# Moving VectorE's mask of a level in a seven-level block inverse behind the add of the level before, and reordering the work between levels

## What is computed

```
first_block:  h = rms_norm(x, g_mix);  proj = h @ w_in
              y_dsa  = sparse attention, 8 heads of 128, top 64 of 256 keys
              y_rwkv = RWKV-7 recurrence, 16 heads of 64, over 256 steps
              x += concat(y_dsa, y_rwkv) @ w_out;   x += mixture of 16 experts
second_block: layer 0: gated delta rule (8 key heads, 16 value heads of 128) beside
              windowed attention (8 heads);   layer 1: short convolution
              each with its input and output projection, then a final norm
```

## Time and profile before

| what | value |
|---|---|
| median of the runs | 3404.0 us |
| the profiled execution's own time | 3401.54 us |
| its span, first to last instruction | 3399.8 us |
| PE (TensorE matmul) busy | 3102.0 us, 91% |
| PEld (weight load) busy | 2872.3 us, 84% |
| DVE (VectorE) busy | 2021.8 us, 59% |
| ACT (ScalarE) busy | 1547.8 us, 46% |
| mean granted TensorE clock | 0.971 of 2.4 GHz |

### The profile page before, as it was taken

The page is one execution under the profiler, slowest core; times in us unless marked ns, Lnnn a source line. Parts: engine busy times, 40 slices in busy tenths (PEclk is TensorE's granted clock), DMA queues, the critical chain, the costliest instruction groups (busy, mean ns, idle before and its releaser), DMA issues.

```text
span 3399.8 us, 59603 instructions
## 1 busy us (share of the span) xinstructions
PE 3102.0 (91%) x22592; PEld 2872.3 (84%) x22592; DVE 2021.8 (59%) x2817; ACT 1547.8 (46%) x2121; POOL 77.9 (2%) x98
## 2 busy tenths in 40 slices
PE   7988888869899999999798898989979899999998
PEld 6877777759799977777688888888869899999998
DVE  5766555544555688888555655656544555555544
ACT  4443333323444477767444443444424444444443
POOL 0000000001000000000000000000001000000001
PEclk9999999979999999999899999999989999999999
DMA  5422222204556699999333333334325455555554
GB/s 190 140 95 83 82 85 86 88 29 137 155 158 183 201 345 326 349 323 361 117 118 112 126 114 114 120 111 130 109 71 181 153 181 181 182 178 178 182 182 138
DMA packets 231154, 543.78 MB, mean 160 GB/s; under 512 B 16768, under 2 KB 98944, under 8 KB 231040
## 3 DMA queue, kind: packets, MB, share of 16 engines
q1 hardware_dynamic: 229664, 537.99, 47.8%
q0 software_dynamic: 656, 2.49, 0.2%
q10 hardware_dynamic: 720, 1.74, 0.1%
HBM read 540.05 MB, written 2.10 MB: 159 GB/s over the span
## 4 chain that ended last, share of the span: by engine, by line
PE 53%; issue 29%; DVE 11%; ACT 6%; DVEq 1%; POOL 0%; DMA 0%; ACTq 0%; POOLq 0%; SPq 0%
PE gp L431 14%; PE gp L432 14%; PE gp L433 14%; ACT w_hi L1050 3%; PE pm L484 2%; DVE arena L1690 2%; PE pm L478 2%; DVE w_lo L1516 1%; DVE arena L2018 1%; PE pm L470 1%; DVE arena L1535 1%; DVE arena L1681 1%; PE pm L970 0%; DVE h_both L1528 0%; PE pm L980 0%
## 5 line engine op out<-in xcount | busy, mean ns | idle before, releaser
L1516 DVE TENSOR_TENSOR w_lo<-stage,w_hi 128x1024 fp32r<-128x1024 f32 x1018 | 1238.7, 1224 | 923.7 <-ACT w_hi L1050 908.7
L1050 ACT ACTIVATE w_hi<-stage 128x1024 fp32r<-128x1024 f32 x1018 | 1071.5, 1057 | 860.0 <-PE gp L433 646.9
L431 PE MATMUL gp<-h_both,w_hi 128*128 128x256 f32 x4432 | 1301.4, 294 | 48.7 <-DVE w_lo L1516 19.7
L432 PE MATMUL gp<-h_both,w_hi 128*128 128x256 f32 x4432 | 1264.1, 285 | 0.0
L433 PE MATMUL gp<-h_both,w_lo 128*128 128x256 f32 x4432 | 1263.3, 285 | 0.0
L431 PEld LDWEIGHTS gp<-h_both,w_hi 128*128 128x128 f32 x4432 | 861.1, 194 | 72.7 <-issue 32.8
L432 PEld LDWEIGHTS gp<-h_both,w_hi 128*128 128x128 f32 x4432 | 861.5, 194 | 2.4 <-issue 1.7
L433 PEld LDWEIGHTS gp<-h_both,w_lo 128*128 128x128 f32 x4432 | 859.9, 194 | 0.0
L431 PE MATMUL gp<-y_both,w_hi 128*128 128x256 f32 x1024 | 292.2, 285 | 0.4 <-DVE y_both L1528 0.4
L432 PE MATMUL gp<-y_both,w_hi 128*128 128x256 f32 x1024 | 291.5, 285 | 0.0
L433 PE MATMUL gp<-y_both,w_lo 128*128 128x256 f32 x1024 | 291.4, 285 | 0.0
(11 more groups left out here) (468 smaller groups left out, 3451.8 us busy)
## 6 DMA issues: line engine op xcount, KB each, us to landing
stage<-in_stream SPq DMA_DIRECT2D x1018, 512.0 KB, 4.0
x<-in_x SPq DMA_DIRECT2D x4, 512.0 KB, 8.7
out<-arena SPq DMA_DIRECT2D x4, 512.0 KB, 2.6
arena<-in_lora POOLq DMA_DIRECT2D x8, 192.0 KB, 2.7
c<-in_c POOLq DMA_DIRECT2D x1, 896.0 KB, 4.8
c<-in_c ACTq DMA_DIRECT2D x1, 704.0 KB, 10.3
c<-in_c ACTq DMA_DIRECT2D x1, 640.0 KB, 7.8
vecs<-in_vecs ACTq DMA_DIRECT2D x1, 184.0 KB, 5.4
```

The source lines that it names most:

```text
L431: T.matmul(o, w_hi[:, slot, w], hi[:, k, :], start=first[t], stop=False)
L432: T.matmul(o, w_hi[:, slot, w], lo[:, k, :], start=False, stop=False)
L1050: A.activation(w_hi[:, slot, :], stage[:, k, :], ACT.Copy).then_inc(s_hi, 1)
L1516: V.tensor_tensor(w_lo[:, slot, :], stage[:, sub % SLOTS, :], w_hi[:, slot, :].bitcast(F32), ALU.subtract).then_inc(s_lo, 1)
```

## The change

VectorE's mask of level lv + 1 is issued right behind its add of level lv (`masked`), before anything else. RWKV's mask of level 0 moves ahead of the masks of R and the normed q and k; the delta rule's stays where it was, behind the same wait. What VectorE does between levels (`slot`) now stands behind that mask: in RWKV the splits stand in levels 2, 4 and 6 in place of 1, 3 and 5, ahead of `dsa(lv)`; in the delta rule they stay in 1, 3 and 5, but behind the add. The product of the cosine with q and k (line 1655) moves from `dsa(1)` to `dsa(0)`. TensorE turns the probabilities in level 6 between the turning of Y and the product (`dsa_turned`), no longer at the end of level 5. In the delta rule the two tiles at place 1 move to place 3 (`EIGHTH2`). ScalarE's program is unchanged. No instruction that computes is added or removed.

```diff
@@ -470,7 +470,7 @@
                     ins = T.transpose(o, i_, ident)
                 ins.then_inc(s, 1)
 
-            def inverse(first, state, N, C, C0, it, fill, after=None):
+            def inverse(first, state, N, C, C0, it, fill, mid=None, after=None):
 
                 for lv in range(7):
                     pe.wait_ge(s_inv, 9 * it + lv + 1)
@@ -478,6 +478,8 @@
                         ins = T.transpose(pm[:, 0, s_ * P:(s_ + 1) * P], (state if lv else first)[:, s_, :], ident)
                     ins.then_inc(s_trn, 1)
                     fill(2 * lv)
+                    if lv == 6 and mid is not None:
+                        mid()
                     pe.wait_ge(s_trno, 7 * it + lv + 1)
                     pe.wait_ge(s_blk, 7 * it + lv + 1)
                     for s_ in range(4):
@@ -488,7 +490,8 @@
                     if after is not None:
                         after(lv)
 
-            EIGHTH = {0: 0, 1: 1, 2: 2, 4: 3, 5: 4, 6: 5, 7: 6, 8: 7, 9: 8, 10: 9, 11: 10, 12: 11}
+            EIGHTH1 = {at: q for q, at in enumerate([0, 1, 2, 4, 5, 6, 7, 8, 9, 10, 11, 12])}
+            EIGHTH2 = {at: q for q, at in enumerate([0, 2, 3, 4, 5, 6, 7, 8, 9, 10, 11, 12])}
 
             pe.wait_ge(s_zero, 1)
 
@@ -542,8 +545,8 @@
                     feed(n, i, U_T1, 6, EV_T1, tiles)
 
             def feed1_eighth(at, i, last):
-                if at in EIGHTH:
-                    q = EIGHTH[at]
+                if at in EIGHTH1:
+                    q = EIGHTH1[at]
                     feed1(5 + q // 4, i, last, (q % 4 * 2, q % 4 * 2 + 2))
 
             def dsa(lv, i):
@@ -562,15 +565,16 @@
                         ins = T.matmul(pm[:, 4, qt * S:(qt + 1) * S], d_qk[:, 0, qt * P:(qt + 1) * P], d_qk[:, 1, :],
                                        start=True, stop=True)
                     ins.then_inc(sem("s_ds_sc"), 1)
-                if lv == 5:
-                    pe.wait_ge(sem("s_at_pr"), i + 1)
-                    transposes([(pm[:, 3, kt * S + qt * P:kt * S + (qt + 1) * P], d_pr[:, qt, kt * P:(kt + 1) * P])
-                                for kt in range(NT) for qt in range(NT)], sem("s_at_pT"))
                 if lv == 6:
                     pe.wait_ge(sem("s_at_pTo"), i + 1)
                     for kt in range(NT):
                         ins = T.matmul(pm[:, 4, 0:S], d_v[:, kt, :], d_pT[:, kt, :], start=kt == 0, stop=kt == NT - 1)
                     ins.then_inc(sem("s_at_o"), 1)
+
+            def dsa_turned(i):
+                pe.wait_ge(sem("s_at_pr"), i + 1)
+                transposes([(pm[:, 3, kt * S + qt * P:kt * S + (qt + 1) * P], d_pr[:, qt, kt * P:(kt + 1) * P])
+                            for kt in range(NT) for qt in range(NT)], sem("s_at_pT"))
 
             def rwkv(p, last=False):
                 pe.wait_ge(sem("s_rw_lw"), 16 * p + 16)
@@ -619,7 +623,7 @@
                     if at == 2:
                         pe.wait_ge(sem("s_rw_R"), 2 * p + 2)
 
-                inverse(r_Y, r_Y, r_N, r_C, r_C, p, fill, lambda lv: dsa(lv, p))
+                inverse(r_Y, r_Y, r_N, r_C, r_C, p, fill, lambda: dsa_turned(p), lambda lv: dsa(lv, p))
                 pe.wait_ge(s_inv, 9 * p + 9)
                 for c in range(NT):
 
@@ -893,8 +897,8 @@
                     feed(n, i, U_T2, 12, EV_T2, tiles)
 
             def feed2_eighth(at, i, last):
-                if at in EIGHTH:
-                    q = EIGHTH[at]
+                if at in EIGHTH2:
+                    q = EIGHTH2[at]
                     feed2(9 + q // 4, i, last, (q % 4 * 2, q % 4 * 2 + 2))
 
             def delta(i, last=False):
@@ -1650,9 +1654,11 @@
 
             def dsa(lv, i):
 
+                if lv == 0:
+                    dve.wait_ge(sem("s_ds_qn"), i + 1)
+                    V.tensor_tensor(d_t1, d_qn, bc(con("cos_q"), 2), ALU.mult)
                 if lv == 1:
                     dve.wait_ge(sem("s_at_rot"), i + 1)
-                    V.tensor_tensor(d_t1, d_qn, bc(con("cos_q"), 2), ALU.mult)
                     link(V.tensor_tensor(d_t2, pm[:, 3, :].rearrange("p (a b) -> p a b", a=2), bc(con("sin_q"), 2), ALU.mult))
                     V.tensor_tensor(d_qk, d_t1, d_t2, ALU.add).then_inc(sem("s_at_qk"), 1)
                     dve.wait_ge(sem("s_at_vT"), i + 1)
@@ -1673,13 +1679,12 @@
                     lower(y_lo[:, i, :], y_hi[:, i, :], pm[:, 4, 0:S], s_y)
 
 
-            def solver(Y, N, it, between, after=None, turned_first=False):
+            def masked(Y, N, it, lv):
+                dve.wait_ge(s_inv, 9 * it + lv + 1)
+                V.tensor_tensor(N, Y, bc(levels[:, lv, :], 4), ALU.mult).then_inc(s_blk, 1)
+
+            def solver(Y, N, it, slot):
                 for lv in range(7):
-                    dve.wait_ge(s_inv, 9 * it + lv + 1)
-                    if lv == 0 and turned_first:
-                        dve.wait_ge(s_trno, 7 * it + 1)
-                    V.tensor_tensor(N, Y, bc(levels[:, lv, :], 4), ALU.mult).then_inc(s_blk, 1)
-                    between(lv)
                     if lv == 6:
                         dve.wait_ge(s_inv, 9 * it + lv + 1)
                         dve.wait_ge(s_trn, 7 * it + lv + 1)
@@ -1688,8 +1693,9 @@
                     dve.wait_ge(s_inv, 9 * it + lv + (2 if lv == 6 else 1))
                     dve.wait_ge(s_prod, 7 * it + lv + 1)
                     V.tensor_tensor(Y, Y, pm[:, 1, :].rearrange("p (a b) -> p a b", a=4), ALU.add).then_inc(s_inv, 1)
-                    if after is not None:
-                        after(lv)
+                    if lv < 6:
+                        masked(Y, N, it, lv + 1)
+                    slot(lv)
 
             def rwkv(p, last=False):
                 for j in range(3):
@@ -1746,6 +1752,7 @@
                     ins = V.tensor_tensor(r_Aak[:, 2 * hd:2 * hd + 2, :], pm[:, hd, S:2 * S].rearrange("p (a b) -> p a b", a=2),
                                           bc(con("strict"), 2), ALU.mult)
                 ins.then_inc(sem("s_rw_R"), 1)
+                masked(r_Y, r_N, p, 0)
                 for hd in range(2):
                     dve.wait_ge(sem("s_rw_mR"), 2 * p + hd + 1)
                     ins = V.tensor_tensor(r_R[:, hd, :, :], pm[:, (2, 4)[hd], :].rearrange("p (a b) -> p a b", a=4),
@@ -1755,7 +1762,13 @@
                 V.scalar_tensor_tensor(d_qn[:, 0, :], d_raw[:, 0, :], vec("q_gain"), d_rs[:, 0:S], ALU.mult, ALU.mult)
                 V.scalar_tensor_tensor(d_qn[:, 1, :], d_raw[:, 1, :], vec("k_gain"), d_rs[:, S:2 * S], ALU.mult,
                                        ALU.mult).then_inc(sem("s_ds_qn"), 1)
-                solver(r_Y, r_N, p, lambda lv: feed1(5 + lv // 2, p, last) if lv % 2 else None, lambda lv: dsa(lv, p))
+
+                def slot(lv):
+                    if lv in (2, 4, 6):
+                        feed1(4 + lv // 2, p, last)
+                    dsa(lv, p)
+
+                solver(r_Y, r_N, p, slot)
                 feed1(8, p, last)
                 dve.wait_ge(sem("s_rw_mS"), p + 1)
                 for hd in range(2):
@@ -2058,7 +2071,9 @@
                 ins.then_inc(sem("s_dn_kd"), 1)
                 feed2(8, i, last)
 
-                solver(n_Y, n_N, i + RWKV_P, lambda lv: feed2(9 + lv // 2, i, last) if lv % 2 else None, turned_first=True)
+                dve.wait_ge(s_trno, 7 * (i + RWKV_P) + 1)
+                masked(n_Y, n_N, i + RWKV_P, 0)
+                solver(n_Y, n_N, i + RWKV_P, lambda lv: feed2(9 + lv // 2, i, last) if lv % 2 else None)
                 feed2(12, i, last)
 
                 dve.wait_ge(sem("s_dn_mks"), i + 1)
```

## The result

The changed kernel takes 3325.06 us (median of four runs, 3324.39 to 3326.84) against 3405.16 for the one before (four runs; the 3404.0 ahead was the median of three); the ratio of the runs is 0.9766, 95% interval 0.9749 to 0.9783. The forecast was 3331 and the profiled execution, at 3324.39 with a span of 3322.7, is 77.1 us shorter in its span than the one before.

A forecast was written before the change was run, and what follows sets the result against it. Over half the chain of waits is TensorE, idle mainly in the inverses, where VectorE's order can matter. Gains 44 + 3 + 20.9 + 4.8 = 73 us from 3401.5 give 3328.5, plus 2.5 for the median: 3331, range 3318 to 3356.

The forecast's parts named there:

- The undisturbed level: One inverse level with nothing in the way: 3.26 us in RWKV, 3.28 in the delta rule; anything above can be gained.
- The terms in an RWKV turn: Gains per level of RWKV's inverse, less a loss behind it: 6.3 us a turn, 44 over seven turns with feeds.
- Level 6: RWKV inverse, level 6: 3.92 us against 4.51, gain 0.6, with a new wait of about 0.6 before the probabilities.
- Behind the inverse: RWKV, after the last add: a split of 1.23 us before the attention output's low half, about 0.3 showing as loss.
- Turns 2, 4 and 6: RWKV turns with clock drops behind the level 1 to 2 stretch: three drops taken as gone, 4.8 us.
- Turn 7: RWKV turn without splits, clock at 0.67: only the masks count, 3 us taken, between 0 and 6.3.
- The delta rule: Its inverse's three odd levels lose a split's delay of 0.87 us each, over eight turns: 20.9; level 6 costs 0.
- Cosine product, moved fills: Cosine product in level 0's idle time; two delta tiles from place 1 to 3 fit before Y: nothing.
- A: Rival: inverse gains come, but clock drops stay (3336) or come in each turn with feeds (3355); chance 0.2.
- B: Rival: waits move to VectorE in RWKV levels 2, 4 and 6, half its gain given back, 3353; chance 0.08.
- C: Rival: levels held by ScalarE's copy and TensorE's fills alone, moved masks only change names, 3404; chance 0.03.
- D: Rival: slower, denser inverses fall to 1.2 GHz and stay there, at most 3643; chance 0.03.

The follow-up runs named there:

- Experiment two: Kernel before, with ScalarE alone rounding the halves in levels 0, 2 and 4 of both inverses, not 1, 3 and 5: 3362.53 us, ratio 0.9882.
- experiment one: Kernel before, with only the delta rule's VectorE splits of levels 1, 3 and 5 put behind add and next mask: 3383.46 us, ratio 0.9950.
- experiment ten: Changed kernel with last split behind the low half, scores moved into level 3, and probabilities divided ahead of level 6's mask in RWKV: 3315.84 us.
- six: Changed kernel with the cosine product moved back from level 0 to level 1: 3324.38 us, ratio 0.9766.
- seven: Changed kernel with the delta rule's two fill tiles back at place 1: 3324.88 us, ratio 0.9763.
- experiment three: Changed kernel with RWKV's splits in the slots of levels 1, 3 and 5 in place of 2, 4 and 6: 3336.33 us, ratio 0.9801.

## Why the prediction was right, point by point

**The undisturbed level** of 3.26, put together from 2.09 and 1.17, came out at 3.29, and the delta rule's at 3.29 for 3.28.

**The terms in an RWKV turn.** Level 0: 1.26 forecast, 1.22 measured (first add 21.53 and 20.31 us into the turn). Level 1: 0.89 and 0.86. Level 2: 1.5 and 1.49. Level 3: 0.88 and 0.87. Levels 4 and 5: 1.54 and 1.50. Level 6: 0.6 and 0.65, the wait in front of the probabilities not 0.6 but 0.3, since the fill of that place stands in it. Behind the inverse: 0.3 forecast as lost, 0.28 measured (2.01 to 2.29). Sum 6.3 forecast (the terms add up to 6.37) and 6.3 measured (74.3 to 67.98).

**Turns 2, 4 and 6.** Each lost 7.9 us, 6.3 and the 1.6 of the clock drop (a short stretch at 1.2 GHz): the 4.8 came. The reason I gave is not borne out, so this term was right by luck. I put the drop down to the stretch from level 1 to level 2 with its late mask. But the same stretch of turn 3 of the kernel before is just as idle as the one of turn 2 in the earlier trace rows, and no drop follows it:

```profile
411.90:417.90 6.00, 3.87 (x25) 2.73 (x24) 4.65 (x7) 1.76 (x3) 0.00 (x0) 1.00 0.26 87
```

Experiment two keeps the late mask, with a wait of 1.78, and has no drop in these turns (72.0 each, and 71.7 for turn 6, which is 0.3 shorter in the changed kernel too). With the RWKV part of the kernel before unchanged (experiment one) the drops stay, and turn 0 has one more. So something besides this stretch decides, the density of the inverse or where it falls in time, and the runs don't tell which.

**Turn 7** was mis-sized: 3 forecast, 7.0 measured. As an estimate, the order is worth the 3: the first add comes 0.5 earlier in the turn (21.29 to 20.80), and the inverse, first to last add, fell from 26.8 to 23.5, of which level 2 gave 1.14, level 4 0.63 and level 6, by what it gave in the other turns, 0.65 (levels 1, 3 and 5, without a split here, nothing). The other 4 is clock: a drop in level 6 that is gone (0.9), and 3.2 behind the inverse. The stretch from the last add to the output of the turn, before and after:

```profile
736.76:756.30 19.54, 15.91 (x67) 13.25 (x67) 3.39 (x8) 3.57 (x10) 0.00 (x0) 0.59 0.00 0
683.94:700.20 16.26, 12.71 (x67) 10.21 (x66) 3.40 (x8) 3.57 (x10) 0.00 (x0) 0.76 0.00 1
```

That share moves from kernel to kernel; in experiment ten turn 7's inverse ran in 20.2 us at a clock of 1.00. I had the bounds (0 to 6.3) from the masks alone and left its clock out.

**The delta rule.** The term 0.87 for an odd level was right (0.86: 4.15 to 3.29), and level 6's row of four VectorE instructions cost nothing (3.35 before, 3.36 now). The inverses gained 2.6 us a turn. Over seven turns that is 18.1, and the ledger has 15.9. The 2.2 was lost outside the inverse, which the sum had unchanged. There every turn has a clock drop, at TensorE's 4 us wait in the windowed attention, and in some turns it lasts twice as long. Windows of the kernel before, from the last add of one turn's inverse to the first of the next, in two neighbouring turns:

```profile
1748.20:1833.80 85.60, 78.61 (x597) 74.78 (x598) 52.48 (x91) 40.73 (x68) 2.56 (x2) 0.96 0.40 127
1856.20:1940.80 84.60, 77.67 (x597) 73.82 (x598) 52.44 (x91) 40.73 (x68) 2.56 (x2) 0.98 0.40 128
```

and of the changed kernel:

```profile
1791.40:1877.10 85.70, 78.50 (x594) 74.46 (x594) 52.48 (x92) 40.73 (x68) 2.55 (x2) 0.96 0.41 134
```

At 0.96 the stretch takes 85.3 to 86.0 us, at 0.98 84.0 to 84.8. Before, the two kinds alternated, four long and three short; after the change five in a row are long, with a short one on either side. One long one more is worth about 1 us. The rest is that the long stretches took 85.3 to 85.6 us before and take 85.7 to 86.0 after; why isn't shown. That the drops may fall differently was in the range (4 us), not in the sum.

**Cosine product, moved fills**: both costed at nothing, both worth nothing (six, seven). For the first I had then expected 0.3 in its own run, and overlooked what the sum itself said of level 3, that TensorE begins it behind the scores.

**The rivals.** A, drops that stay or come in every turn: not seen inside the inverse of any turn with feeds; outside it the delta rule's got longer, as above. The rule of the Trainium skill that I weighed, from "TensorE: Matmul & The Clock Gate", section "A second HAM failure mode: psum-queue depth-cycling", does not show up here: the inverse of delta turn 1, with its matmuls busy for 18.57 of 19.80 us, ran at a granted clock of 1.00, and so did those of RWKV turns 0 to 6 and of all other delta turns. As the pauses left are this short, the runs don't say where the rule would begin. B: the levels came out as forecast, so nothing was given back; experiment three shows what it would have looked like. C: no, the adds themselves moved. D: the clock in the inverses with feeds is 1.00.

**The total.** The profiled execution was to take 3328.5 and took 3324.4. The 4.1 are: turn 7, 4.0 more gain; 2.8 between the stages and 1.6 in turns 0 to 6 (turn 0's own clock drop shrank) that I hadn't counted (between the stages the mean clock rose only from 0.97 to 0.98, and how much of the 2.8 that explains is open); less 2.7 in the delta rule and 1.3 ahead of turn 0; the rest is rounding. The median of the runs lies 0.7 above the profiled execution, not the 2.5 that I added: 1.8 more. So of the 5.9 between 3331 and 3325.06 the largest part, turn 7's 4, is clock, 1.8 is the distance of the median from the profiled execution, and no part is a level of the inverse in a turn with feeds. Gains and losses of 1 to 4 us that the sum did not have partly cancel: that the total came this close is partly luck, the terms of the turns are not.

## What to carry to other kernels

In a loop of short dependent steps over several engines, measure one step that nothing disturbs and compare every other with it; the differences are the sum, and they were right here to 0.1 us in the turns that have feeds. When an add is late behind a piece of side work, ask first for what that piece waits: starting its input earlier on another engine can be worth as much as reordering the engine that is late. And a wait in front of independent work (the probabilities, the scores) belongs in the shadow of another engine's step, behind the instruction that starts that step, not in front of it.

## What the runs showed of the hardware that wasn't expected

The clock drops of TensorE moved with edits that leave the stretch ahead of them as it was. RWKV turns of 74.3 and 75.9 took turns in the kernel before, though the 6.0 us ahead of the drop hold 3.87 or 3.88 us of matmuls in both kinds; experiment one, with the same RWKV instructions, had a further drop in turn 0; and the edit on ScalarE, which left a wait of 1.8 us in each turn, made turns 1 to 5 all 72.0. What decides isn't shown. In turn 7, which has no feeds, the inverse took 26.8, 23.5 and 20.2 us in the kernel before, the changed one and experiment ten. The first step is some 2.4 of order and 0.9 of clock, the second 2.8 of clock (levels 1 and 2 took 4.75 and 4.83, mostly at 1.2 GHz, and then 3.37 and 3.36 at 2.4) and 0.5 of order, in level 6. A comparison by medians can move by several microseconds for this reason, which is why the small edits above were judged by the turns.
